# Writing the scan's closing sums as 64x64 matmuls instead of 64x128 ones

## What is computed

```python
def step(S, inp):
    r_t, w_t, kk_t, b_t, k_t, v_t = inp
    S = (S * w_t[..., None, :]
         - jnp.einsum('dbhvk,dbhk->dbhv', S, kk_t)[..., None] * b_t[..., None, :]
         + v_t[..., None] * k_t[..., None, :])
    return S, jnp.einsum('dbhvk,dbhk->dbhv', S, r_t)
```

## Time and profile before

| | |
|---|---|
| median of three runs | 2525.96 us |
| profiled execution: its own time | 2525.96 us |
| profiled execution: span from first to last instruction | 2524.2 us |
| PE busy over the span | 2158.9 us (86%) |
| DVE, ACT, POOL busy | 51%, 36%, 29% |
| scan stage: first and last `z` | 753 us, 1200 us from the span's start |
| mean granted clock of PE | 0.923 of full speed |

### The profile page before, as it was taken

One profiled execution on the slowest core, in us unless ns is written; L12 is line 12 of the kernel. 1 busy time (PEld: TensorE's weight loads), 2 busy tenths in 40 slices (PEclk: granted clock), 3 DMA queues, 4 the chain that ended last, 5 costly groups with the idle time before them and its releaser, 6 DMA issues. The chain is left out here.

```text
span 2524.2 us, 57280 instructions
## 1 busy us (share of the span) xinstructions
PE 2158.9 (86%) x24254; PEld 1823.0 (72%) x24254; DVE 1291.5 (51%) x2064; ACT 905.5 (36%) x1765; POOL 723.2 (29%) x786
## 2 busy tenths in 40 slices
PE   3899997798179999998699994993899969999988
PEld 1666885576169989998588884773787758888866
DVE  4335467976435555554354444975546424444322
ACT  2223144455245555553133332223333303333311
POOL 2246322211143342431050001443457415000012
PEclk6999998899589999999699996996999979999989
DMA  8555444553422122110421106534344453111062
GB/s 300 184 145 155 132 146 147 187 175 120 149 77 79 54 79 78 55 58 16 96 92 34 43 13 195 182 115 162 109 114 103 112 140 117 51 51 51 32 205 92
DMA packets 207036, 280.46 MB, mean 111 GB/s; under 512 B 39640, under 2 KB 145016, under 8 KB 205760
## 3 DMA queue, kind: packets, MB, share of 16 engines
q1 hardware_dynamic: 168736, 171.52, 22.4%
q0 software_dynamic: 25680, 81.58, 10.2%
q10 hardware_dynamic: 12368, 23.70, 3.1%
HBM read 188.78 MB, written 87.95 MB: 110 GB/s over the span
## 5 line engine op out<-in xcount | busy, mean ns | idle before, releaser
L164 PE MATMUL in_acc<-in_hi,in_whi 128*128 128x512 f32 (+1 forms) x1024 | 401.3, 392 | 19.9 <-DVE in_lo L840 17.9
L164 PE MATMUL in_acc<-in_lo,in_whi 128*128 128x512 f32 (+1 forms) x1024 | 380.3, 371 | 0.0
L164 PE MATMUL in_acc<-in_hi,in_wlo 128*128 128x512 f32 (+1 forms) x1024 | 380.1, 371 | 0.0
L164 PEld LDWEIGHTS in_acc<-in_hi,in_whi 128*128 128x128 f32 x1024 | 199.5, 195 | 72.7 <-issue 42.5
L164 PEld LDWEIGHTS in_acc<-in_lo,in_whi 128*128 128x128 f32 x1024 | 199.7, 195 | 35.4 <-issue 5.3
L164 PEld LDWEIGHTS in_acc<-in_hi,in_wlo 128*128 128x128 f32 x1024 | 198.9, 194 | 33.3
L1935 DVE TENSOR_REDUCE dense_top<-dense_score 128x1 f32<-128x640 f32 (+1 forms) x144 | 112.3, 780 | 163.1 <-PE dense_score L2022 163.1
L1935 DVE TENSOR_REDUCE window_top<-window_score 128x1 f32<-128x640 f32 (+1 forms) x128 | 101.2, 791 | 179.5 <-PE window_score L2018 179.5
L2060 PEld LDWEIGHTS dense_outs<-dense_V,dense_p 128*128 128x128 f32 x1344 | 170.3, 192 | 8.5 <-ACT dense_p L1903 4.9
L2060 PE MATMUL dense_outs<-dense_V,dense_p 128*128 128x65 f32 x1344 | 170.7, 270 | 0.9 <-ACT dense_p L1903 0.8
L2060 PE MATMUL window_outs<-window_V,window_p 128*128 128x65 f32 x1216 | 157.6, 273 | 1.6 <-ACT window_p L1903 1.1
(11 more groups left out here) (269 smaller groups left out, 5085.6 us busy)
## 6 DMA issues: line engine op xcount, KB each, us to landing
streams<-in_streams_out POOLq DMA_DIRECT2D x40, 512.0 KB, 3.8
scan_L<-streams SPq DMA_DIRECT2D x80, 256.0 KB, 3.7
in_wl<-in_w_mod ACTq DMA_DIRECT2D x32, 512.0 KB, 4.4
in_raw<-in_w_in_even SPq DMA_DIRECT2D x28, 512.0 KB, 4.3
in_raw<-in_w_in_odd SPq DMA_DIRECT2D x20, 512.0 KB, 3.8
close_ga<-gates SPq DMA_DIRECT2D x18, 512.0 KB, 4.3
in_wm<-in_w_mod SPq DMA_DIRECT2D x8, 1024.0 KB, 12.2
gates<-in_outs POOLq DMA_DIRECT2D x32, 256.0 KB, 3.5
```

Source lines behind the costliest of these rows:

```text
L164: last = pe.matmul(out, a(k), b(k), start=(k == 0 and x == 0), stop=(k == n - 1 and x == 2))
```

## The change

Each matmul of `z` with 128 output partitions becomes two with 64: `o` picks the first or the second 64 columns of the stationary operand and the same half of the output's partitions. The values and the order of the sums are the same. The number of matmuls in one `z` rises from 24 to 48 in the program, 48 to 96 in MATMUL rows; over 20 groups with two `z` each, 960 become 1920 in the program.

```diff
                                     u, half = unit(h, d, g), half_of(x ^ d)
-                                    to = sums[d][:, x, h * 2 + g, :]
-                                    if n == 0:
-                                        pe.matmul(to, U[j % 4][half, u, 0, :], PD[s][half, u, HD:P], start=True, stop=False)
-                                    elif n == 1:
-                                        pe.matmul(to, U[j % 4][half, u, 1, :], values_of(j, u, half), start=False, stop=False)
-                                    else:
-                                        last = pe.matmul(to, EQ[s][half, u, :], state[half, d, r, h * 2 + g, :], start=False, stop=True)
+                                    for o in range(2):
+                                        to, cols = sums[d][half_of(o), x, h * 2 + g, :], half_of(o)
+                                        if n == 0:
+                                            pe.matmul(to, U[j % 4][half, u, 0, cols], PD[s][half, u, HD:P], start=True, stop=False)
+                                        elif n == 1:
+                                            pe.matmul(to, U[j % 4][half, u, 1, cols], values_of(j, u, half), start=False, stop=False)
+                                        else:
+                                            last = pe.matmul(to, EQ[s][half, u, cols], state[half, d, r, h * 2 + g, :],
+                                                             start=False, stop=True)
                     last.then_inc(z_in, 1)
```

## The result

The change makes the kernel slower: 2560.95 us against 2533.35 us, medians of 19 runs each on the same chips, a ratio of 1.0116 (95% interval 1.0099 to 1.0134). The forecast was 2472. In the profiles the last MATMUL row of `z` starts at 1200.2 us before and at 1230.2 after, and the first at 753.1 and 752.7: the scan is 30 us longer, close to the 27.6 us between the medians. The profiled execution after took 2570.19 us, 44 above the one before; the other 14 us of it lie in windowed attention, whose code is the same. I come back to them at the end.

What follows compares the result with a forecast made beforehand. PE was taken to bound the scan, except at one wait ahead of `first`. Saving 60.4 us on z, less 2.5 for stalls and 4 for lost cover, gave 54 us: 2472 us from 2525.96, range 2461 to 2490.

Steps and rivals of the forecast that it cites:

- What a z costs: Each z in the scan: 0.117 us a product instead of 0.224, 1.48 us a z, 60.4 us saved in all.
- Rival A: In z, the two halves of a product sharing rows don't overlap: z 2.81 us, 2521 us in total; chance 0.08.
- Can PE be fed so fast: PE's instruction supply in the scan: one packet in 3.1 us, far from 1.09; added stalls cost 2.5 us.
- my 20.9: Forecast length in us of one scan period after the change, down from 23.9.
- The term for stalls: Scan: 3,840 more instructions are 15 packets, giving two or three more stalls of 1 us: 2.5 us.
- One stall in each period: PE's waits for "issue" before the change: four of 0.9 us mean in a row, about one each period.
- The clock: PE's granted clock in the scan: all z but the last run at full clock; no loss was forecast.
- What is late next: Waits behind the shorter z on ACT, DVE and POOL: 4 us lost, 8 if cover goes in every period.
- (a) to (c): Behind z: x_of still starts after ACT's copy; the chain to first keeps 4.92 us; DVE's EQ delays the new state 0.55.
- (c): DVE's EQ delays x_new some 0.4 us inside PE's idle 0.70 before first; stalls hidden there lose cover, 4 us.
- Rival C: Accumulating quarters of z run one after another: 0.47 us a product, z 5.6 us, 2631 us in total; chance 0.04.
- issue becoming several in each period: Stated sign that the prediction is wrong: PE's stalls for instructions become several in each scan period.

Runs made afterwards that it cites:

- e3: The change for z(j, 1) alone, z(j, 0) left whole as in the kernel before: 2562 us, 1.0109 of the kernel before.
- e13: The change for z(j, 0) alone, z(j, 1) left whole as in the kernel before: 1.0041 of the kernel before.
- e12: Kernel before, z whole, with y_of, first, av and x_of in half as many matmuls of 128 streamed columns (other values): 2515 us.
- e17: The change with all stream loads issued later in the period, behind av: 2.0% slower than the kernel before.
- e6: The change with stream loads of 16 instead of 512 columns from the third group on (other values): 0.5% slower than the kernel before.

## Why the prediction was wrong

Step by step. **What a z costs** was right: 0.117 us a product, no extra time at entry, and 60 us less work in the scan. Rival A, the neighbours in the same rows, did not come. The Trainium skill's rule that spoke for it (TensorE: Matmul & The Clock Gate, The mechanism) is not borne out where it would have kept the second neighbour's weight load from overlapping the first one's matmul: four rows of a round share two row halves and still follow a round every 0.0586 us.

**"Can PE be fed so fast"** is the step that failed. It set the distance of packets (4.0 us) against the time that one takes to move (1.09 us) and called 3.1 "still far from 1.09". The time of moving is no bound: the shortest distance from 780 to 1150 us is 3.3 us, and it stood in the trace of before (3.35), where I didn't look for the minimum. 1,706 instructions are 6.7 packets of 254, times 3.3 at the least 22.2 us a period, so my 20.9 could not be reached. That bound alone would still have promised a gain on 23.9. The period came to 26.3 us, 3.93 a packet, since PE's work is uneven, with one packet ahead at most, and packets wait behind the loads. The term for stalls, 2.5 us, was in truth 76 us of pauses. "One stall in each period" was noted and priced, but by one row of the waits (3.6 us of 8.7) and as a rate per instruction, not as the sign that a supply was at its edge.

**The clock** was the second term, put at nothing: "all but the last run at the full clock" was true before, and the prediction kept it for the change without a reason. With the long pauses it fell to half for 31 us, 14 us of the loss. So the 60 us saved stand against 76 and 14: the scan became 30 us longer in place of 60 shorter.

**What is late next**, (a) to (c), looked at semaphores only. I weighed what the freed time would collide with on ACT, DVE and POOL, but not that the shorter `z(j, 1)` took away the sparse stretch in which the supply caught up beside the loads (e3 against e13). Of (c), that a stall may hide in the wait for `XT`, e12 shows the reverse side: with the stalls gone the scan had as many us of pauses as before. **Rival C** had the right side and the wrong mechanism: no product takes 0.248 us. That something would come out slower had a chance of 0.04 for that mechanism alone, so it was no forecast of this result. The sentence on stalls for "issue becoming several in each period" is what came.

The 14 us of the profiled execution behind the scan: windowed attention took 348 us before and 362 after, with the same instructions, and PE ran at half its clock for 20 and 57 us of them. Over the experiments' profiles that stage took 347 to 383 us, with 20 to 108 us at half the clock, the most of both in e17. So the clock sets its length; what lowers the clock there stays open. Each kernel has one profiled execution, so how much of this the medians carry isn't known; the change's median granted clock is 0.916 and before's 0.920.

## What to carry to other kernels

Before splitting a matmul into more and smaller ones, divide PE's instructions in the stretch by its time and compare with the instruction queue: its smallest distance between packets, not the time that one is under way, is the bound, and each f32 matmul here counts as four instructions. If PE's waits already name "issue" once in a period, the stretch is at the edge, and a shorter sparse step gives its time back at the next packet's end. Then look at the granted clock behind the longest pauses: here it made the loss larger than the pauses were. A matmul that fills half the array in one instruction can be worth more than two quarters that run beside each other.

## What the runs showed of the hardware

- Instructions for PE come in packets of 16 KB, 3.24 to 3.45 us apart at the closest from 780 to 1150 us in every run that has pauses for "issue" there, and PE goes on some 1.4 us behind the landing (1.0 to 1.6 over the 49 such pauses of the change). The next packet starts at least 1.07 us behind PE's going on. The Trainium skill (Runtime: NRT & Kernel Launch, Instruction fetch mechanics) describes blocks of 256 instructions, as here, and calls the cost of crossing from one to the next mostly hidden; this trace has 64 us of it in 370.
- A packet waits behind other transfers on full DMA engines: distances of 5.0 to 5.8 us beside the stream loads, 7.83 once, and none over 4.47 in the change with small loads (e6).
- Each of the eight stretches at half the clock in the change's scan begins within 1 us of the end of a pause of 2.2 to 3.5 us; with no pause over 2 us, before, there is none until 1198 us.
- Quarters of the array overlap fully when neighbours share their rows, and when they accumulate: 0.117 us for two rounds of four, 0.0586 a round.
- One f32 matmul that streams 128 columns costs PE less than two of 64: 0.87 against 0.93 us for a `y_of`.
